# Expert loop of a two-layer hybrid backbone: gate and up product by quarters of the feed-forward columns, and block transposes on VectorE in place of TensorE's

## The reference, cut to what matters

```python
def expert_choice_ffn(h, w_router, w_gate, w_up, w_down):   # once for 128 context rows, once for 512 latent rows
    aff = softmax(xs @ w_router)
    gates, idx = lax.top_k(aff.T, cap)             # cap = 2 n / 16: 16 context rows and 64 latent rows for each expert
    xe = xs[idx]
    hid = silu(einsum('ecd,edf->ecf', xe, w_gate)) * einsum('ecd,edf->ecf', xe, w_up)
    ye = einsum('ecf,efd->ecd', hid, w_down) * gates[..., None]
    out = zeros_like(xs).at[idx.reshape(-1)].add(ye.reshape(-1, D))
```

## Time and profile before

| | us |
|---|---|
| Median of three runs | 1945.66 |
| Lowest and highest run | 1944.28 and 1947.69 |
| Profiled execution: span from first to last instruction | 1945.3 |
| TensorE busy | 1828.2 (94%) |
| VectorE busy | 650.7 (33%) |
| ScalarE busy | 377.7 (19%) |
| GpSimd busy | 200.8 (10%) |
| DMA, mean over the span | 271 GB/s, 526.51 MB |

### The profile page before, as it was taken

One profiled execution on the slowest core, in us unless ns is written; L12 is line 12 of the kernel. 1 busy time (PEld: TensorE's weight loads), 2 busy tenths in 40 slices (PEclk: granted clock), 3 DMA queues, 4 the chain that ended last, 5 costly groups with the idle time before them and its releaser, 6 DMA issues. The chain is left out here.

```text
span 1945.3 us, 34714 instructions
## 1 busy us (share of the span) xinstructions
PE 1828.2 (94%) x14950; PEld 872.5 (45%) x14950; DVE 650.7 (33%) x1394; ACT 377.7 (19%) x904; POOL 200.8 (10%) x275
## 2 busy tenths in 40 slices
PE   5999989959999999999999999999599999999996
PEld 2455655422434343444455566554233434343443
DVE  2345885350212121212243457833411212121211
ACT  2224653120000000000032255421110000000000
POOL 1004300000000000000010331000000000000000
PEclk9999999978999999999999999999799999999998
DMA  9750022237999999999995202031489999999993
GB/s 386 290 227 1 1 106 110 85 137 270 388 396 407 399 410 397 413 396 412 398 355 203 101 1 74 33 152 65 172 334 396 402 398 409 395 414 397 413 385 100
DMA packets 56201, 526.51 MB, mean 271 GB/s; under 512 B 12046, under 2 KB 13694, under 8 KB 26142
## 3 DMA queue, kind: packets, MB, share of 16 engines
q1 hardware_dynamic: 49134, 501.44, 63.8%
q0 software_dynamic: 6336, 21.63, 4.7%
q10 hardware_dynamic: 672, 2.62, 0.3%
HBM read 503.91 MB, written 24.38 MB: 272 GB/s over the span
## 5 line engine op out<-in xcount | busy, mean ns | idle before, releaser
L625 PE MATMUL PS<-arena,xe 128*32 128x512 f32 x6144 | 673.0, 598 | 3.8 <-DVE xe L1444 3.8
L625 PEld LDWEIGHTS PS<-arena,xe 128*32 128x32 f32 x6144 | 195.9, 111 | 457.7 <-issue 453.4
L1455 DVE TENSOR_TENSOR RA<-RA,PS 96x512 f32<-96x512 f32 (+2 forms) x96 | 63.2, 684 | 649.5 <-ACT RA L1147 646.8
L649 PE MATMUL PS<-arena,hdT 128*32 128x512 f32 x1536 | 265.9, 594 | 7.2 <-DMA arena<-w_exp 5.4
L651 PE MATMUL PS<-arena,hdT 128*32 128x256 f32 x1024 | 263.6, 380 | 0.0
L693 PE MATMUL PS<-arena,RB 128*128 128x512 f32 (+1 forms) x480 | 183.5, 530 | 0.0
L654 PE MATMUL PS<-arena,hdT 128*32 128x256 f32 x1536 | 156.0, 379 | 0.0
L655 PE MATMUL PS<-arena,hdT 128*32 128x256 f32 x512 | 152.3, 379 | 0.0
L1147 ACT ACTIVATE RA<-PS 96x512 f32<-96x512 f32 x32 | 19.0, 593 | 672.8 <-PE PS L625 672.8
L1035 PE MATMUL PS<-arena,RB 128*128 128x512 f32 x320 | 138.9, 593 | 0.0
L651 PEld LDWEIGHTS PS<-arena,hdT 128*32 128x32 f32 x1024 | 109.9, 110 | 27.1
(11 more groups left out here) (293 smaller groups left out, 1816.1 us busy)
## 6 DMA issues: line engine op xcount, KB each, us to landing
arena<-w_exp SPq DMA_DIRECT2D x192, 2048.0 KB, 12.8
arena<-ada_rest SPq DMA_DIRECT2D x16, 2048.0 KB, 8.0
ada<-ada_first SPq DMA_DIRECT2D x8, 2048.0 KB, 22.9
arena<-w_in SPq DMA_DIRECT2D x4, 2048.0 KB, 10.8
arena<-w_out SPq DMA_DIRECT2D x2, 4096.0 KB, 13.4
arena<-w_in SPq DMA_DIRECT2D x4, 1536.0 KB, 22.9
RC<-x_res SPq DMA_DIRECT2D x2, 2560.0 KB, 10.6
x_res<-RC SPq DMA_DIRECT2D x10, 512.0 KB, 2.6
```

What stands on the lines that cost most here:

```text
L625: last = mm(PS[GRP * q:GRP * (q + 1), c * 512:(c + 1) * 512], xe[:, k, GRP * grp:GRP * (grp + 1)], w[:, col_, :], start=(k == 0), stop=(k ...
L649: mm(PS[GRP * q:GRP * (q + 1), 1536:2048], tok(q), w[:, 0:512], start=first, **flags)
L1455: V.tensor_tensor(h_, h_, up, ALU.mult).then_inc(hm_rdy.sem, 1)
```

## The change

- **Gate and up product.** The host now packs the weights of a slice as four quarters of 512 columns, each 256 gate columns with the 256 up columns that belong to them. Strip q of the array takes quarter q for every group g of rows, and the product of group g lies in PSUM bank g. So each partition has gate and up parts side by side; SiLU is one instruction over 128 partitions x 768 elements, and so is the multiplication.
- **Hidden tile.** One VectorE block transpose (32 x 32 blocks, within each group of 32 partitions) writes hdT straight from hid (hidden_turned). The rows of the down weights are permuted on the host to match it. It waits for the previous down product (dn_used), and SiLU of the next expert waits for it (hd_rdy). The functions hidden and hidden_in are gone.
- **Rows.** From the second expert on, 12 VectorE block transposes bring the gathered rows from xg to a new tile xq (tokens_turned), and scale and shift work from there. The first expert of a layer still goes through TensorE (first_tokens). GpSimd's next gather waits for xq_rdy.
- **Order.** TensorE's loop is now gate_up(e), down(e-1), and gate_up waits for the multiplication of the expert before (hm_rdy). VectorE's loop is tokens_turned(e+1), column(e+2), times_up(e), tokens_in(e+1), hidden_turned(e), rows_out(e-1).

```diff
--- before
+++ after
@@ -175,7 +175,9 @@
         ys = RA[0:SLOT, D:2 * D]
-        hid = RA[:, 2 * D:2 * D + MAIN]
+        hid = RA[:, 2 * D:2 * D + MAIN].rearrange("p (g c) -> p g c", g=3)
+        xq = RA[:, 4 * D:4 * D + KD * PAD].rearrange("p (j s) -> p j s", j=KD)
+        xg_rows = RA[0:PAD, 0:D].rearrange("p (j c) -> p j c", j=KD)
         g2r = RA[0:SLOT, 3 * D:4 * D]
@@ -352,13 +354,13 @@
         landed = Signal("landed", EXP, primed=True)
-        xT_ps = Signal("xT_ps", EXP + 1)
+        xT_ps = Signal("xT_ps", 1)
+        xq_rdy = Signal("xq_rdy", EXP)
         xe_rdy = Signal("xe_rdy", EXP + 1)
...
         dn_used = Signal("dn_used", 2 * EXP, primed=True)
-        sg_rdy = Signal("sg_rdy", 3 * EXP)
-        hm_rdy = Signal("hm_rdy", 3 * EXP)
-        ht_ps = Signal("ht_ps", EXP)
+        sg_rdy = Signal("sg_rdy", EXP)
+        hm_rdy = Signal("hm_rdy", EXP)
         hd_rdy = Signal("hd_rdy", EXP)
@@ -605,9 +607,9 @@
-            def tokens_in(l, e):
-                n = l * (EXP + 1) + e
-                pe.wait_ge(gathered.sem, n * 16 + 16)
+            def first_tokens(l):
+
+                pe.wait_ge(gathered.sem, l * (EXP + 1) * 16 + 16)
                 for k in range(8):
@@ -619,21 +621,12 @@
                     w = gate_up_weights(k)
-                    for c in range(3):
+                    for g in range(3):
                         for q in range(4):
-                            grp, col_ = (q, c) if q < 3 else (c, 3)
-                            last = mm(PS[GRP * q:GRP * (q + 1), c * 512:(c + 1) * 512], xe[:, k, GRP * grp:GRP * (grp + 1)],
-                                      w[:, col_, :], start=(k == 0), stop=(k == KD - 1), skip_group_check=True)
+                            last = mm(PS[GRP * q:GRP * (q + 1), g * 512:(g + 1) * 512], xe[:, k, GRP * g:GRP * (g + 1)],
+                                      w[:, q, :], start=(k == 0), stop=(k == KD - 1), skip_group_check=True)
                     if k % 2:
                         last.then_inc(gu_used.sem, 1)
-
-            def hidden(E):
-
-                pe.wait_ge(hm_rdy.sem, 3 * E + 3)
-                for j in range(6):
-                    o = 2560 + j * P if j < 4 else (6 + j - 4) * 512 + 384
-                    last = nc.tensor.transpose(PS[:, o:o + P], hid[:, j * P:(j + 1) * P], ident[:, :])
-                last.then_inc(ht_ps.sem, 1)
@@ -1081,19 +1074,14 @@
                 pe.wait_ge(g2_rdy.sem, g2_rdy.at(l, 1))
-                tokens_in(l, 0)
+                first_tokens(l)
                 gate_up(l, 0, l * EXP)
-                tokens_in(l, 1)
-                pe.wait_ge(xe_rdy.sem, xe_rdy.at(l, 2))
-                hidden(l * EXP)
                 with pe.Fori(1, EXP) as e:
                     E = l * EXP + e
+                    pe.wait_ge(hm_rdy.sem, E)
                     gate_up(l, e, E)
-                    pe.wait_ge(hd_rdy.sem, E)
-                    tokens_in(l, e + 1)
                     down(E - 1)
-                    pe.wait_ge(xe_rdy.sem, l * (EXP + 1) + (e + 2))
-                    hidden(E)
+                pe.wait_ge(hm_rdy.sem, hm_rdy.at(l, EXP))
                 if l + 1 < LAYERS:
@@ -1144,21 +1132,9 @@
                 act.wait_ge(gu_used.sem, 4 * E + 4)
-                A(hid[0:PAD, 0:512], PS[0:PAD, 0:512], ACT.Silu).then_inc(sg_rdy.sem, 1)
-                A(hid[0:PAD, 512:MAIN], PS[0:PAD, 1024:1024 + REST], ACT.Silu).then_inc(sg_rdy.sem, 1)
-                A(hid[PAD:P, :].rearrange("p (g c) -> p g c", g=3),
-                  PS[PAD:P, 0:1536].rearrange("p (g c) -> p g c", g=3)[:, :, 0:REST], ACT.Silu).then_inc(sg_rdy.sem, 1)
-
-            def hidden_in(E):
-
-                act.wait_ge(ht_ps.sem, E + 1)
-                low = bank(5).rearrange("p (j s) -> p j s", j=4)
-                high = PS[:, 3072:4096].rearrange("p (j s) -> p j s", j=2)[:, :, 384:512]
-                A(hdT[:, 0:4, :], low[:, :, 0:PAD], ACT.Copy)
-                A(hdT[:, 4:6, :], high[:, :, 0:PAD], ACT.Copy)
-                for g in range(2):
-                    A(hdT[:, 6:8, GRP * g:GRP * (g + 1)], low[:, 2 * g:2 * g + 2, PAD:P], ACT.Copy)
-                A(hdT[:, 6:8, 2 * GRP:PAD], high[:, :, PAD:P], ACT.Copy).then_inc(hd_rdy.sem, 1)
+                if not isinstance(E, int) or E:
+                    act.wait_ge(hd_rdy.sem, E)
+                A(hid, PS[:, 0:1536].rearrange("p (g c) -> p g c", g=3)[:, :, 0:REST], ACT.Silu).then_inc(sg_rdy.sem, 1)
@@ -1375,11 +1351,8 @@
                 silu_gate(l * EXP)
-                hidden_in(l * EXP)
                 with act.Fori(1, EXP) as e:
-                    E = l * EXP + e
-                    silu_gate(E)
-                    hidden_in(E)
+                    silu_gate(l * EXP + e)
@@ -1432,27 +1405,48 @@
-            def tokens_in(ch, l, e):
-
-                n = l * (EXP + 1) + e
-                dve.wait_ge(xT_ps.sem, n + 1)
+            def first_tokens(ch, l):
+
+                dve.wait_ge(xT_ps.sem, xT_ps.at(l, 1))
+                scaled(ch, xT_view)
+
+            def scaled(ch, place):
+
                 for i, (m, op) in enumerate(((amp2[:, :, :], ALU.mult), (mod[:, 24:32, :], ALU.add))):
...
                         v = m[:, :, st:st + 1].rearrange("p (b j) s -> p b j s", b=2).broadcast_to([P, 2, 4, w])
-                        rows = xT_view[:, :, :, a:a + w]
+                        rows = place[:, :, :, a:a + w]
                         out = xe[:, :, a:a + w].rearrange("p (b j) s -> p b j s", b=2) if i else rows
...
+            def tokens_turned(l, e):
+
+                dve.wait_ge(gathered.sem, (l * (EXP + 1) + e) * 16 + 16)
+                dve.wait_ge(xe_rdy.sem, l * (EXP + 1) + e)
+                for g in range(3):
+                    for q in range(4):
+                        ins = V.transpose(xq[GRP * q:GRP * (q + 1), :, GRP * g:GRP * (g + 1)],
+                                          xg_rows[GRP * g:GRP * (g + 1), :, GRP * q:GRP * (q + 1)])
+                ins.then_inc(xq_rdy.sem, 1)
+
+            def tokens_in(ch, l, e):
+
+                dve.wait_ge(xq_rdy.sem, l * EXP + e)
+                scaled(ch, xq.rearrange("p (b j) s -> p b j s", b=2))
+
             def times_up(E):
-                rest = PS[PAD:P, 0:1536].rearrange("p (g c) -> p g c", g=3)[:, :, REST:512]
-                hrest = hid[PAD:P, :].rearrange("p (g c) -> p g c", g=3)
-                for i, (h_, up) in enumerate(((hid[0:PAD, 0:512], PS[0:PAD, 512:1024]),
-                                              (hid[0:PAD, 512:MAIN], PS[0:PAD, 1024 + REST:1536]), (hrest, rest))):
-                    dve.wait_ge(sg_rdy.sem, 3 * E + (i + 1))
-                    V.tensor_tensor(h_, h_, up, ALU.mult).then_inc(hm_rdy.sem, 1)
+                dve.wait_ge(sg_rdy.sem, E + 1)
+                V.tensor_tensor(hid, hid, PS[:, 0:1536].rearrange("p (g c) -> p g c", g=3)[:, :, REST:512], ALU.mult).then_inc(hm_rdy.sem, 1)
+
+            def hidden_turned(E):
+
+                dve.wait_ge(hm_rdy.sem, E + 1)
+                dve.wait_ge(dn_used.sem, 2 * E + 1)
+                V.transpose(hdT[:, :, :].rearrange("p b (g s) -> p g b s", g=3),
+                            hid.rearrange("p g (b r) -> p g b r", r=GRP)).then_inc(hd_rdy.sem, 1)
@@ -1887,18 +1881,22 @@
                 column(first, l, 0, 1, idx_g[:, :], idx_rdy)
-                tokens_in(first, l, 0)
+                first_tokens(first, l)
                 column(first, l, 1, 1, idx_g[:, :], idx_rdy)
+                tokens_turned(l, 1)
+                column(first, l, 2, 1, idx_g[:, :], idx_rdy)
                 times_up(l * EXP)
                 tokens_in(first, l, 1)
-                column(first, l, 2, 1, idx_g[:, :], idx_rdy)
+                hidden_turned(l * EXP)
                 first.end()
...
                     loop.start(l * (EXP - 1) + e - 1)
+                    tokens_turned(l, e + 1)
+                    column(loop, l, e + 2, 1, idx_g[:, :], idx_rdy)
                     times_up(E)
                     tokens_in(loop, l, e + 1)
-                    column(loop, l, e + 2, 1, idx_g[:, :], idx_rdy)
+                    hidden_turned(E)
                     rows_out(l, e - 1, E - 1)
@@ -2025,7 +2023,10 @@
-                    pool.wait_ge(xT_ps.sem, l * (EXP + 1) + e)
+                    if isinstance(e, int) and e == 1:
+                        pool.wait_ge(xT_ps.sem, xT_ps.at(l, 1))
+                    else:
+                        pool.wait_ge(xq_rdy.sem, l * EXP + e - 1)
                     pool.wait_ge(idx_rdy.sem, idx_rdy.at(l, 1) + e)
@@ -2082,8 +2083,8 @@
     u = w_up.reshape(n, 4, 2, P, FF).transpose(0, 1, 3, 2, 4)
-    d = w_down.reshape(n, 2, 4, P, D).transpose(0, 1, 3, 2, 4).reshape(n, 2, P, 4096)
-    gu = np.concatenate([g[..., 0:512], u[..., 0:512], g[..., 512:MAIN], u[..., 512:MAIN], g[..., MAIN:], u[..., MAIN:]], axis=-1)
+    d = w_down.reshape(n, 4, KD, GRP, D).transpose(0, 2, 1, 3, 4).reshape(n, 2, 4, P, D).transpose(0, 1, 3, 2, 4).reshape(n, 2, P, 4096)
```

(1 more changed line is left out.)

## The result

| | before | after |
|---|---|---|
| median of 4 runs each | 1946.68 us (1944.28 to 1948.24) | 1928.59 us (1925.18 to 1931.38) |
| ratio | | 0.990 (interval 0.9879 to 0.9920) |
| profiled execution: span | 1945.3 (no time beside it) | 1928.1 (its time: 1929.82) |
| layer 0: first gate and up product to the first of layer 1 | 958.0 | 957.5 |
| layer 1: its first gate and up product to the end | 949.7 | 931.9 |

What follows compares the result with a forecast made beforehand. TensorE and the DMA engines were both taken as full, TensorE setting the pace until the slack is used up, then DMA at 32.7 us per expert. Gains 5.4 + 5.4 + 13.1 = 23.9 us gave 1921.8 us, range 1908 to 1938.

Steps and rivals of the forecast that it cites:

- TensorE's period: Expert loops: without the 14 transposes TensorE's pass falls from 32.74 to 31.0 us, 1.74 us per expert.
- The block transposes: VectorE, behind the down product: twelve at 415 ns and hidden_turned at 960 ns, 5.0 + 1.0 us, hidden under gate and up.
- the rival of a bound on VectorE: Expert loops: slow block transposes make VectorE the bound from 1.6 us each; at 2.5 us each, 2295 us; chance 6%.
- The transfers' 32.7 us per expert: Expert loops: weights 29.3 us plus gather and scatter 3.4 us, needed however fast TensorE is.
- The rival that had room in the DMA engines: Both loops: the DMA share overstates, TensorE sets the pace throughout, gain 56 us, total 1889; chance 9%.
- Layer 1: Layer 1 gains 13.1 us of slack of expert 14's second down slab, plus 5.4 us from the transfer stream.
- 5.4 of the stream: Each layer: the transfer stream moves earlier by entry 2.0, gather 1.9 and filling 1.5 us; bounds -2 and 9.
- the step behind it: Layer's end: last down product starts 3.6 us after the one before; 1.0 us later, but costs nothing (bound 1.0).
- Layer 0: Layer 0 has no slack to take at its end and gains only the transfer stream's own 5.4 us.
- the entry's 2.0: Loop entry, per layer: a shorter chain from SiLU to the next product releases the first reload 2.0 us earlier (bounds 0, 4).
- The gather's 1.9: Each layer: expert 3's gather is issued before the queue is full and leaves the full stretch, 1.9 us (bounds 0, 1.9).
- filling: First two periods of each layer's loop, below 405 GB/s: closer releases win back 1.5 us (bounds -2, 3.1).

Runs made afterwards that it cites:

- the kernel with small matmuls: Changed kernel plus fifty small matmuls on a constant tile while TensorE waits for layer 0's last down slab: 1926.84 us, ratio 0.9903.

## Why the prediction was right, and where it was not

- **TensorE's period**: 31.0 said, 30.96 measured. **The block transposes**, costed by a copy and a multiplication: 435 and 978 ns, hidden. Right, and the rival of a bound on VectorE had no ground: 11.59 us of 30.96.
- **The transfers' 32.7 us per expert**: late passes at 32.5 to 32.7. Right, and the switch came near the tenth expert. The rival that had room in the DMA engines (1889) is about what the runs gave once bytes were taken away, 1889.08 and 1892.63, and only then.
- **Layer 1**: 18.5 us said (13.1 of slack, 5.4 of the stream), 17.7, 16.5 and 15.6 measured. In the profile of after the second down slab of expert 14 lands at 1866.7 + 25.2 = 1891.9, against 1897.4. Layer 1 also began 0.5 us later, so the stream moved 6.0 (4.7 and 4.5 in the other two profiles); and the product that used up that slab ended at 1898.0 in place of 1915.7:

```profile
L482 SPq DMA_DIRECT2D arena<-w_exp x2: 338/338/339, 1892.8 to 1898.0; - x2
DMA to landing us min/median/max: 7.6/8.6/9.6
```

  That is 17.7 us earlier, with 18.5 said, and right within a microsecond in that execution. The traces show where the rest went, in three small pieces. The stream's term is 0.3 too large in the mean. The product ends 6.0 to 6.1 us after the second slab's landing in all three profiles, where the prediction counted 5.2: the slab that it hangs on is the first of the two, which landed at 1860.4 + 26.7 = 1887.1, only 4.8 us ahead of the second:

```profile
L482 SPq DMA_DIRECT2D arena<-w_exp x2: 332/332/333, 1860.4 to 1866.7; - x2
DMA to landing us min/median/max: 25.2/25.9/26.7
```

  And the step behind it was costed at nothing. The last down product starts 3.89 us after the one before it (3.6 said, 1.89 before) and runs partly at the lower clock, 0.50 from 1903 to 1905:

```profile
1901.81 1.06 PE L642 MATMUL PS<-arena,hdT 128*32 128x512 f32 x3 [3.89 <-DVE RA L1462]
```

  From the end of the one product to the end of the other it takes 16.2, 16.2 and 17.0 us in the three profiles, and 15.6 before. No run tried to win this back.
- **Layer 0**: 5.4 us said; 0.5, 5.5 and 2.8 measured, 2.9 in the mean. The stream itself moved by 3.4, 7.4 and 5.5 (table), 5.4 in the mean, and 4.5 with the 1.7 of the kernel with small matmuls. So the size of the term was about right; that the mean of three meets it so closely is luck. The step that failed is what was made of it: "Layer 0 gains only what the stream of transfers itself gains" took for granted that what the stream gains arrives. TensorE waits 13.50 us for the first of the last two slabs instead of 2.19, and its clock is at the lower level when that slab lands: 2.4 to 3.1 us go there. The prediction had the 2.19-us wait and knew that TensorE would run further ahead; it didn't ask what a wait 11 us longer does to the product behind it. The Trainium skill (TensorE: Matmul & The Clock Gate, "HAM oscillation — how this bites in real kernels") describes such a kernel, in which each product that has waited for its transfer starts at the low clock. The trace agrees for the long wait, with 0.50 from 955 to 970; the product behind the 2.19 us of the kernel before began at full clock, with 0.63 us for three matmuls.
- **The terms of the 5.4**: the entry's 2.0 rests on a chain that became 2.3 us shorter. The gather's 1.9 per layer is not borne out: putting the gather back cost 1.0 for both layers by the medians and nothing by the ratios, though the intervals are too wide to exclude 3.8. How the sum divides between entry, gather and filling is not shown.
- **The sum**: 23.9 said, 18.1 measured (19.3 and 17.1 in the later jobs). By the mean of the three profiles layer 0 is 2.5 short of its 5.4 and layer 1, at 16.6, is 1.9 short of its 18.5; over both layers the three executions gain 18.2, 22.0 and 18.3 on the one profile of the kernel before.

## What to carry to other kernels

Where two resources are nearly balanced, work taken off one of them buys about the slack of the other (in layer 1 here 13.1 us of 26), and what its stream gains besides (some 5): compute what each needs per period, and the slack at the place where the period ends, before counting engine time. The sign of the coming limit was not a share near 1 but an issue-to-landing time that grows from pass to pass. And where an engine gets far ahead of its transfers, ask what that longer wait does to it, and which load lands right behind the one that it waits for; both can swallow a gain that the stream has really made. Before a load is moved behind another one, look at when that other one can be issued: here the same reordering was harmless where the queue was long and left it empty for some 5 us where it was short.

## What the runs showed of the hardware that was not expected

- The DMA share read 0.99 at 373 GB/s with slabs that landed in 8 to 12 us, and 1.01 at 404 with landings of 27 us. It doesn't tell a full queue from one with room.
- Putting two 2048-KB loads behind two slabs changed nothing where slabs landed 27 us after issue, and cost 9.5 us where they landed after 14.
- A wait of 13.5 us left TensorE at 1.2 GHz for the first 5 us of the next product, and one of 4.49 us did the same; a wait of 3.76 us behind 11.4 us of small matmuls still did so for part of them; and one of 3.54 us behind mixed work doubled the eight matmuls after it, from 3.60 to 7.19 us. Behind waits of 2.19 and 2.16 us the product began at full clock.
- One pass with the block transposes of the rows on VectorE and one with them on TensorE differ by 0.84 us (30.96 and 31.80).
